# A hybrid decoder layer on one core: modulation and h in two halves of the model's columns, with ten column tiles summed in pairs

## The chip, the cores and the metric

The kernel runs on one core of a Trainium2 chip. The metric is the device time of one execution in microseconds (us). Five engines work side by side and are tied together by semaphores: the tensor engine (PE), VectorE (DVE), ScalarE (ACT), GpSimd (POOL) and SyncE (SP), which issues the transfers from device memory.

## The reference, cut to what matters

```python
shift, scale, gate = jnp.split(c @ w_ada + b_ada, 3, axis=-1)
h = _rmsnorm(x, g_pre) * (1.0 + scale[:, None, :]) + shift[:, None, :]
z_ssm, xbc, dt_raw, q, kv, nsa_gate, z_att, merge_gate = jnp.split(h @ w_in, IN_SPLITS, axis=-1)
y_ssm = _mamba2_branch(z_ssm, xbc, dt_raw, ...) @ w_ssm_out
y_nsa = _nsa_branch(q, kv, nsa_gate, z_att, ...) @ w_nsa_out
mg = jax.nn.sigmoid(merge_gate.reshape(bsz, s, N_BRANCH, dm))
merged = mg[:, :, 0] * y_ssm + mg[:, :, 1] * y_nsa
return x + gate[:, None, :] * _rmsnorm(merged @ w_out, g_post)
```

x has 256 rows of 1024 columns. The Mamba branch passes x, B and C through a causal convolution of four taps, and runs the chunked state-space sum (SSD) over 32 heads in four groups. The attention branch compresses keys and values (kc, vc) in overlapping blocks through a small MLP, and adds a full attention.

## The kernel before

**Units.** Every weight matrix is cut into units of 128 x 1024 floats (512 KB), 133 of them, in the order of `weight_units()` (L35): first dtg (dt and the attention gates), b0 to b3, c0 to c3, then four times four x tiles and four z tiles, then kc0, kc1, vc0, vc1, then za and the weights of the compression (w1k, w1v), and so on. SyncE copies the units one after the other into seven slots w_raw (L492).

**The split.** A product in full precision is made of three faster ones. ScalarE casts a unit to w_hi (L847, `split_hi`), VectorE takes w_raw - w_hi for the first six or seven of the eight pieces (L1096, `split_lo`), and GpSimd for the rest (L1415). h is split likewise into h_hi and h_lo. `weight_unit()` (L572) then gives, for each of the eight pieces k of h's columns, three products: h_hi x w_hi (L621), h_lo x w_hi (L622), h_hi x w_lo (L623). So a unit is 24 products. Splits run three units ahead (`AHEAD`).

**The sums** of a column tile lie in one of three PSUM banks (gemm0 to gemm2) in rotation. Four more kinds of bank exist: score0, score1, small0, small1 and y_or_o.

**The start.** SyncE issues params, the first constants, then the eight pieces of w_ada for shift and scale (L476, 1 MB each, a piece is 128 rows of the model) with x after the second, then two units. The tensor engine sums the squares of x over the columns (L523), multiplies c by each piece as it lands (L531), and transposes the four rows of 512 results (L536), which ScalarE has copied (L934). VectorE makes shift (L1212) and scale (L1214); h is then made piece by piece: h_hi on ScalarE (L939), h on VectorE (L1218) or, for k = 2, 4, 6, on GpSimd (L1405), and h_lo on VectorE (L1226). All eight pieces of w_ada must have landed before any of h exists.

**The order** is written out by hand. `schedule()` (L64) puts named steps behind units; `put(10, ("acs", 0))` puts step acs behind unit 10. The tensor engine and GpSimd follow STEPS, ScalarE and VectorE follow LATE_STEPS, in which the steps behind a unit come one unit later. A finished tile is read out one unit later, too: for b, c and x that is one ScalarE operation (L881), three of VectorE's (L1144), a tanh (L890) and a product (L1105). The steps that count here:

- dtT, dtA, dtE, dtB, dtL, dtC: dt from dtg, in small operations on several engines; GpSimd's last chain is dtC (L1449 to L1457), and acs (L644) on the tensor engine waits for its result, adt.
- xt, seg, ea, y (L700, L703), ysq, ysum, ssq, yn: the SSD of a group and its norm, from unit 17 + 8g on for group g.
- blk (L463, `compress_blocks`): the overlapping blocks of kc on VectorE (behind unit 48) and of vc on GpSimd (behind 47), 16 operations each. The first w1k product (L595) waits for kc's.

## Time and profile before

| | |
|---|---|
| median of 3 runs | 485.87 us (485.31 to 487.09) |
| profiled execution | 486.2 us, its span 484.4 us |
| PE busy | 447.9 us (92%) |
| DVE / ACT / POOL busy | 350.6 / 266.9 / 228.9 us |
| granted clock, mean | 0.981 of full speed |
| moved | 82.99 MB, mean 171 GB/s |

The span runs from the first to the last instruction of the profiled execution. Busy is the time in which an engine had an instruction under way; matmuls overlap, so their own durations (0.28 us) are longer than the distance between two of them. The granted clock tells how much of TensorE's 2.4 GHz was given: 1.00 or 0.50 (1.2 GHz) at any one time.

### The profile page before, as it was taken

Reading aid. Unit: us, or ns where it says so; the run is one execution under the profiler, and the core shown is the slowest. Engines: PE = TensorE matmul, PEld = TensorE weight load, DVE = VectorE, ACT = ScalarE, POOL = GpSimd, SP = SyncE. Lnnn points to the kernel's source line nnn. Section 1 sums busy time; section 2 is a strip of 40 time slices with the busy share of each in tenths; the row PEclk is TensorE's granted clock in tenths of the full one; section 3 lists DMA queues with packets and bytes.
Section 4 is the critical chain, followed back from the end, with each engine's and each line's share of the span. In section 5 each row is a group of like instructions: output and inputs, shape, how many; then the busy total and the mean of one; then the engine's idle time right before and its main releaser. Section 6 shows DMA issues by size and latency. Waiting matters only on the chain.

```text
span 484.4 us, 9763 instructions
## 1 busy us (share of the span) xinstructions
PE 447.9 (92%) x3592; PEld 409.6 (85%) x3592; DVE 350.6 (72%) x611; ACT 266.9 (55%) x518; POOL 228.9 (47%) x238
## 2 busy tenths in 40 slices
PE   0759989999999979997999999999999999999995
PEld 0439989999999879995889999889898999999874
DVE  0167989698999988979775676668696766549633
ACT  1354776555585584635587744656565464535441
POOL 0043453358477746988255552244355353344340
PEclk9987999999999998999999998999999999999999
DMA  8996544733534226144719740625747433356102
GB/s 319 425 385 221 173 132 146 217 117 131 177 127 169 96 93 213 45 175 148 264 62 360 259 169 1 246 76 201 262 140 248 137 101 130 120 178 243 58 2 87
DMA packets 21959, 82.99 MB, mean 171 GB/s; under 512 B 2444, under 2 KB 2834, under 8 KB 20626
## 3 DMA queue, kind: packets, MB, share of 16 engines
q1 hardware_dynamic: 21912, 82.37, 48.1%
q8 instruction: 29, 0.48, 0.4%
q14 instruction: 18, 0.15, 0.1%
HBM read 81.31 MB, written 1.05 MB: 170 GB/s over the span
## 4 chain that ended last, share of the span: by engine, by line
PE 72%; DVE 7%; issue 7%; ACT 5%; DMA 5%; POOL 3%; SPq 1%; DVEq 0%; POOLq 0%; ACTq 0%
PE gemm L621 18%; PE gemm L622 17%; PE gemm L623 17%; DMA w_raw<-in_wpack 5%; PE y_or_o L818 2%; ACT w_hi L847 2%; PE y_or_o L700 2%; ACT probs L1051 1%; DVE w_lo L1096 1%; PE score L782 1%; DVE cmp_blocks L463 1%; PE score L784 1%; SPq L476 1%; PE small L568 1%; PE small L570 1%
## 5 line engine op out<-in xcount | busy, mean ns | idle before, releaser
L1415 POOL TENSOR_TENSOR w_lo<-w_raw,w_hi 128x256 fp32r<-128x256 f32 (+1 forms) x117 | 128.5, 1104 | 171.5 <-ACT w_hi L847 137.4
L621 PE MATMUL gemm<-h_hi,w_hi 128*128 128x256 f32 x680 | 198.1, 291 | 2.4 <-DVE h_lo L1226 2.1
L622 PE MATMUL gemm<-h_lo,w_hi 128*128 128x256 f32 x680 | 192.8, 284 | 0.0
L623 PE MATMUL gemm<-h_hi,w_lo 128*128 128x256 f32 x680 | 192.4, 283 | 0.0
L1096 DVE TENSOR_TENSOR w_lo<-w_raw,w_hi 128x768 fp32r<-128x768 f32 (+1 forms) x117 | 128.9, 1103 | 42.5 <-ACT w_hi L847 41.9
L847 ACT CAST w_hi<-w_raw 128x1024 fp32r<-128x1024 f32 x117 | 122.1, 1045 | 41.8 <-PE gemm L623 27.7
L621 PEld LDWEIGHTS gemm<-h_hi,w_hi 128*128 128x128 f32 x680 | 130.6, 192 | 5.7 <-issue 4.7
L622 PEld LDWEIGHTS gemm<-h_lo,w_hi 128*128 128x128 f32 x680 | 130.6, 192 | 0.6
L623 PEld LDWEIGHTS gemm<-h_hi,w_lo 128*128 128x128 f32 x680 | 130.4, 192 | 0.0
L1144 DVE SCALAR_TENSOR_TENSOR conv_acc<-gemm,conv_half,conv_acc 128x255 f32<-128x255 f32 (+2 forms) x72 | 34.5, 480 | 8.2 <-ACT conv_acc L881 6.2
L621 PE MATMUL gemm<-ynorm_hi,w_hi 128*128 128x256 f32 x128 | 36.6, 286 | 0.0
L623 PE MATMUL gemm<-ynorm_hi,w_lo 128*128 128x256 f32 x128 | 35.8, 280 | 0.0
L622 PE MATMUL gemm<-ynorm_lo,w_hi 128*128 128x256 f32 x128 | 35.8, 279 | 0.0
L881 ACT ACTIVATE conv_acc<-gemm,conv_half 128x256 f32<-128x256 f32 x24 | 13.6, 565 | 32.2 <-PE gemm L623 21.2
L1051 ACT ACTIVATE probs<-score,softmax_small 128x128 f32<-128x128 f32 (+1 forms) x64 | 26.1, 423 | 1.5 <-DVE softmax_small L1333 1.5
L1467 POOL TENSOR_TENSOR cb_decay<-decay,cb_T 128x512 f32<-128x512 f32 x8 | 13.0, 1629 | 27.0 <-ACT decay L990 27.0
L621 PEld LDWEIGHTS gemm<-ynorm_hi,w_hi 128*128 128x128 f32 x128 | 24.0, 188 | 0.7 <-issue 0.7
L1425 POOL TENSOR_TENSOR seg_moving<-acs_rows,consts 128x512 fp32r<-128x512 f32 x16 | 21.7, 1375 | 6.1 <-DVE acs_cols L1259 6.1
L622 PEld LDWEIGHTS gemm<-ynorm_lo,w_hi 128*128 128x128 f32 x128 | 24.1, 188 | 0.0
L623 PEld LDWEIGHTS gemm<-ynorm_hi,w_lo 128*128 128x128 f32 x128 | 24.0, 188 | 0.0
L854 ACT ACTIVATE tanh_tmp<-gemm 128x256 f32<-128x256 f32 x24 | 9.2, 385 | 23.6 <-PE gemm L623 22.8
L1058 ACT COPY probs_T<-small 128x512 f32<-128x512 f32 x16 | 9.5, 593 | 20.6 <-PE y_or_o L818 20.5
(233 smaller groups left out, 778.8 us busy)
## 6 DMA issues: line engine op xcount, KB each, us to landing
w_raw<-in_wpack SPq DMA_DIRECT2D x133, 512.0 KB, 4.0
w_ada_shift_scale<-in_w_ada SPq DMA_DIRECT2D x8, 1024.0 KB, 14.8
x_T<-in_xT SPq DMA_DIRECT2D x1, 1024.0 KB, 10.4
x_residual<-in_x_tok SPq DMA_DIRECT2D x1, 1024.0 KB, 4.9
out_tok_dram<-out_tok SPq DMA_DIRECT2D x4, 256.0 KB, 2.1
...
```

Source lines behind the costliest of these rows:

```text
L621: nc.tensor.matmul(bank[:, 0:SEQ], w_hi, hi[:, k0 + k, :], start=first, stop=False)
L622: nc.tensor.matmul(bank[:, 0:SEQ], w_hi, lo[:, k0 + k, :], start=False, stop=False)
L623: last = nc.tensor.matmul(bank[:, 0:SEQ], w_lo, hi[:, k0 + k, :], start=False, stop=end)
L700: nc.tensor.matmul(bank[64 * k:64 * k + 64, CHUNK * c:CHUNK * (c + 1)], XDT[:, c, h, :], MM[:, c, q4, :], start=True, stop=(c == 0))
L847: nc.scalar.copy(WH[:, n % HI_SLOTS, :], RAW[:, u % RAW_SLOTS, :]).then_inc(hi_ready, 1)
L881: nc.scalar.activation(ACC[:, ci % 2, :], bank, ACT.Identity, bias=CW[:, 96 + col:97 + col], scale=CW[:, 4 * col + 3:4 * col + 4]).then_in ...
L1051: last = nc.scalar.activation(E[:, k, b, P * qt:P * qt + nk], SB[qt][:, nk * b:nk * b + nk], ACT.Exp, bias=SM[:, k, 0, c:c + 1], accum_out ...
L1096: nc.vector.tensor_tensor(WL[:, n % LO_SLOTS, 0:c], RAW[:, u % RAW_SLOTS, 0:c], WH[:, n % HI_SLOTS, 0:c], ALU.subtract).then_inc(lo_ready, 1)
L1144: ins = nc.vector.scalar_tensor_tensor(ACC[:, ci % 2, s:SEQ], GB[t % G_BANKS][:, 0:SEQ - s], CW[:, 4 * col + tap:4 * col + tap + 1], ACC[: ...
L1415: nc.gpsimd.tensor_tensor(WL[:, n % LO_SLOTS, c:1024], RAW[:, u % RAW_SLOTS, c:1024], WH[:, n % HI_SLOTS, c:1024], ALU.subtract).then_inc( ...
L1425: nc.gpsimd.tensor_tensor(MV[:, c, :, :], TP[:, c, :].unsqueeze(1).to_broadcast([P, 4, P]), oh, ALU.mult).then_inc(mv_done, 1)
L1467: nc.gpsimd.tensor_tensor(MM[:, 1, :, :], EX[:, 1, :, :], CB[:, 1, i // 2, :].unsqueeze(1).to_broadcast([P, 4, P]), ALU.mult).then_inc(mm_ ...
```

## The change

Modulation and h are made in two halves of the model's 1024 columns, 512 each. w_ada is laid out so that the first 4 MB give shift and scale of the first half, the second 4 MB those of the second. The squares, the scaling of x, the row sums (32 products of 256 columns for each half, into a half bank of small0), the copy, the transposes and h each come as two calls.

Ten tiles (dtg, b0 to b3, c0, kc0, kc1, vc0, vc1) are taken in five pairs. A pair unit holds for two tiles the weights of one half of the columns: 24 products as in any unit, twelve for each tile. Units 0 to 4 are the pairs' first halves, units 5 to 9 their second halves; their ten sums stay open meanwhile in all banks but small0 (`HOME`, two tiles in one bank where there is a 1). The second half of the modulation (step ada2) stands behind unit 3, its transposes in the middle of unit 4. Then come c1, c2, c3 (units 10 to 12), and x and z from 13 on, four units later than before; kc and vc no longer stand behind the last z. The SSD steps come three units later. The dt steps move too, the blocks of kc and vc are made group by group behind units 18 + 8g (kc, VectorE) and 19 + 8g (vc, GpSimd). In units 5 to 16 a split goes ahead of the read-outs. SyncE issues x first, then alternates. Of h, GpSimd makes k = 2 and 6 only, VectorE k = 4 too. The exponential of a_log and the three casts of constants (L1399 to L1401) move behind other work; the transfer of alibi_k no longer waits for the norm. The number of units, products with h, and bytes is the same.

```diff
+PAIRS = ((("dtg", 0), ("b", 0)), (("kc", 0), ("b", 1)), (("kc", 1), ("b", 2)), (("vc", 0), ("b", 3)), (("vc", 1), ("c", 0)))
+PAIR_READ = (PAIRS[0], (("b", 1),), (("kc", 0), ("kc", 1), ("b", 2)), (("b", 3),), (("vc", 0), ("vc", 1), ("c", 0)))
+HALF_K = KT // 2
+
+
 def weight_units():
 
-    units = [("dtg", 0, 0)]
-    units += [("b", j, 0) for j in range(4)] + [("c", j, 0) for j in range(4)]
+    units = [("pair", i, half) for half in range(2) for i in range(len(PAIRS))]
+    units += [("c", j, 0) for j in range(1, 4)]
     for g in range(SSM_GROUPS):
         units += [("x", TPG * g + j, 0) for j in range(TPG)] + [("z", TPG * g + j, 0) for j in range(TPG)]
-    units += [("kc", j, 0) for j in range(2)] + [("vc", j, 0) for j in range(2)]
-
     units += [("za", j, 0) for j in range(6)]
...
+def tiles_done(u):
+
+    kind, j, part = UNITS[u]
+    if part != LAST_PART.get(kind, 0):
+        return ()
+    return PAIR_READ[j] if kind == "pair" else ((kind, j),)
...
-    put(2, ("dtT", 0))
-    put(4, ("dtA", 0), ("dtE", 0))
-    put(6, ("dtB", 0), ("dtL", 0))
-    put(8, ("dtC", 0))
-    put(10, ("acs", 0))
+    put(len(PAIRS) - 2, ("ada2", 0))
+    put(6, ("dtT", 0))
+    put(7, ("dtA", 0), ("dtE", 0))
+    put(8, ("dtB", 0), ("dtL", 0))
+    put(10, ("dtC", 0))
+    put(13, ("acs", 0))
     for kind in range(3):
-        put(11 + kind, ("cb", kind))
+        put(15 + kind, ("cb", kind))
     ssq_after = 12
     for g in range(SSM_GROUPS):
-        b = 17 + 8 * g
+        b = 20 + 8 * g
...
-    put(47, ("blk", 1))
-    put(48, ("blk", 0))
+    for g in range(KV_GROUPS):
+        put(18 + 8 * g, ("blk0", g))
+        put(19 + 8 * g, ("blk1", g))
+    put(47, ("clear", 0))
...
+HOME = {("dtg", 0): ("gemm0", 0), ("b", 0): ("gemm0", 1), ("b", 1): ("gemm1", 0), ("b", 2): ("gemm2", 0),
+        ("b", 3): ("score0", 0), ("c", 0): ("score1", 0), ("kc", 0): ("small1", 0), ("kc", 1): ("small1", 1),
+        ("vc", 0): ("y_or_o", 0), ("vc", 1): ("y_or_o", 1)}
+SECOND_HALVES = [tile for tile in HOME if HOME[tile][1]]
+FIRST_HALVES = [tile for tile in HOME if tile not in SECOND_HALVES and (HOME[tile][0], 1) in HOME.values()]
+BEFORE, _n = {}, 0
+for _tile in TILE_IDX:
+    if _tile not in HOME:
+        HOME[_tile] = (BANKS[_n % G_BANKS], 0)
+        _n += 1
+    _last = [t for t in TILE_IDX if TILE_IDX[t] < TILE_IDX[_tile] and HOME[t][0] == HOME[_tile][0]]
+    BEFORE[_tile] = _last[-2:] if _last and HOME[_last[-1]][1] == 1 else _last[-1:]
 RAW_SLOTS, HI_SLOTS, LO_SLOTS = 7, 4, 4
-H_POOL = (2, 4, 6)
+H_POOL = (2, 6)
+H_DVE = tuple(k for k in range(KT) if k not in H_POOL)
+EARLY_SPLITS = range(len(PAIRS), 17)
...
-            for k in range(KT):
-                sp.dma_start(ADA[:, k, :], w_ada1[:, k, :]).then_inc(ada_in[k], 16)
-                if k == 1:
-                    sp.dma_start(XT[:], xT).then_inc(x_in, 16)
-            for u in range(2):
-                sp.dma_start(RAW[:, u, :], wpack[u]).then_inc(w_in[u], 16)
+            for s in range(2):
+                sp.dma_start(XT[:, HALF_K * s:HALF_K * (s + 1), :], xT[:, HALF_K * s:HALF_K * (s + 1), :]).then_inc(x_in[s], 16)
+            first_units = len(PAIRS)
+            for n in range(KT):
+                s, k = n // HALF_K, 2 * (n % HALF_K)
+                if n >= HALF_K - 1:
+                    u = n - HALF_K + 1
+                    sp.dma_start(RAW[:, u, :], wpack[u]).then_inc(w_in[u], 16)
+                sp.dma_start(ADA[:, s, k:k + 2, :], w_ada1[:, s, k:k + 2, :]).then_inc(ada_in[n], 16)
             sp.dma_start(CS[:, early:CST["end"][1]], cst_in[:, early:CST["end"][1]]).then_inc(cst2_in_s, 16)
-            for u in range(2, len(UNITS)):
+            for u in range(first_units, len(UNITS)):
...
+            def ada_rows(s):
+
+                for k in range(KT):
+                    if k % 2 == 0:
+                        pe.wait_ge(ada_in[HALF_K * s + k // 2], 16)
+                    for j in range(4):
+                        last = nc.tensor.matmul(ada_sums[32 * j:32 * j + 1, :], par("c", k, k + 1),
+                                                ADA[:, s, k, 256 * j:256 * j + 256], start=(k == 0), stop=(k == KT - 1))
+                last.then_inc(ada_full, 1)
+
+            def ada_columns(s):
+
+                pe.wait_ge(rows_done, s + 1)
+                for m in range(2):
+                    o = 256 * s + P * m
+                    last = nc.tensor.transpose(ada_cols[:, P * m:P * m + P], ROWS[:, o:o + P], ident)
+                last.then_inc(modT_full, 1)
+
             pe.wait_ge(par_in_s, 16)
             pe.wait_ge(bank_zeroed, 1)
-            for k in range(KT):
-                pe.wait_ge(ada_in[k], 16)
-                for j in range(4):
-                    last = nc.tensor.matmul(SB[0][32 * j:32 * j + 1, :], par("c", k, k + 1), ADA[:, k, 512 * j:512 * j + 512],
-                                            start=(k == 0), stop=(k == KT - 1))
-            last.then_inc(ada_full, 1)
-            pe.wait_ge(rows_done, 1)
-            for m in range(4):
-                last = nc.tensor.transpose(SB[1][:, P * m:P * m + P], ROWS[:, P * m:P * m + P], ident)
-            last.then_inc(modT_full, 1)
+            ada_rows(0)
+            ada_columns(0)
...
+                if kind == "pair":
+                    n = SPLIT_IDX[u]
+                    pe.wait_ge(hi_ready, n + 1)
+                    pe.wait_ge(lo_ready, n + 1)
+                    for kk in range(HALF_K):
+                        k = HALF_K * part + kk
+                        if j == 0:
+                            pe.wait_ge(h_ready, k + 1)
+                        if u == len(PAIRS) - 1 and kk == 2:
+                            ada_columns(1)
+                        for m in range(2):
+                            c = 2 * kk + m
+                            if c == lo_share(n):
+                                pe.wait_ge(lo_rest_ready, n + 1)
+                            bank = home(PAIRS[j][m])
+                            w_hi = WH[:, n % HI_SLOTS, P * c:P * c + P]
+                            w_lo = WL[:, n % LO_SLOTS, P * c:P * c + P]
+                            first = k == 0 and PAIRS[j][m] not in SECOND_HALVES
+                            end = k == KT - 1 and PAIRS[j][m] not in FIRST_HALVES
+                            nc.tensor.matmul(bank, w_hi, HH[:, k, :], start=first, stop=False)
+                            nc.tensor.matmul(bank, w_hi, HL[:, k, :], start=False, stop=False)
+                            last = nc.tensor.matmul(bank, w_lo, HH[:, k, :], start=False, stop=end)
+                    last.then_inc(unit_mm, 1)
...
+                elif what == "ada2":
+                    ada_rows(1)
...
+            copy_rows(0)
             split_hi(1)
-
...
+                    split_first = i in EARLY_SPLITS or any(kind == "nsa" for kind, j in done)
+                    if not split_first:
+                        for tile in done:
+                            read_out(tile)
                     if i + AHEAD in SPLIT_IDX:
                         split_hi(SPLIT_IDX[i + AHEAD])
-                    if not late_split:
-                        read_out(done)
-                    done = finished_tile(i)
+                    if split_first:
+                        for tile in done:
+                            read_out(tile)
...
+            scale_x(0)
             split_lo(0)
-
-            dve.wait_ge(modT_full, 1)
-            rows = SB[1][:, :].rearrange("p (m j r) -> p j m r", m=4, j=4)[:, :, :, 0]
-            link(nc.vector.tensor_tensor(MOD[:].rearrange("p (j m) -> p j m", j=4), rows,
-                                         par("b_ada", 0, 16).rearrange("p (j m) -> p j m", j=4), ALU.add))
-            nc.vector.scalar_tensor_tensor(AB[:, 0:8], MOD[:, 8:16], 1.0, par("g_pre"), ALU.add, ALU.mult).then_inc(ab_done, 1)
-            dve.wait_ge(ab_done, 1)
-            for k in range(KT):
-                if k not in H_POOL:
-                    nc.vector.tensor_scalar(HF[:, k, :], XT[:, k, :], AB[:, k:k + 1], MOD[:, k:k + 1], ALU.mult,
-                                            ALU.add).then_inc(h_f32, 1)
-                if k >= 1:
-                    dve.wait_ge(h_hi, k)
-                    if k - 1 in H_POOL:
-                        dve.wait_ge(h_f32_pool, H_POOL.index(k - 1) + 1)
-                    else:
-                        dve.wait_ge(h_f32, k - sum(m < k - 1 for m in H_POOL))
-                    nc.vector.tensor_tensor(HL[:, k - 1, :], HF[:, k - 1, :], HH[:, k - 1, :], ALU.subtract).then_inc(h_ready, 1)
-            dve.wait_ge(h_hi, KT)
-            dve.wait_ge(h_f32, KT - len(H_POOL))
-            nc.vector.tensor_tensor(HL[:, KT - 1, :], HF[:, KT - 1, :], HH[:, KT - 1, :], ALU.subtract).then_inc(h_ready, 1)
-            for n in range(1, AHEAD):
+            make_h(0)
+            split_lo(1)
+            scale_x(1)
+            for n in range(2, AHEAD):
...
+                elif what == "blk1":
+                    pool.wait_ge(lo_rest_ready, made_rest[0])
+                    compress_blocks(pool, nc.gpsimd, 1, i)
+                elif what == "clear":
                     nc.gpsimd.memset(HVR[:], 0.0).then_inc(zeros, 1)
```

**The tensor engine's queue at the start.** First before, the last piece of w_ada and unit 0; then after, where units 3 and 4 meet and unit 5 begins. w_raw, w_hi, w_lo are the weights, small0, score1 and so on are PSUM banks.

```order
L531 MATMUL score0<-w_ada_shift_scale_84,params_60 1x512 [waits ada_in7]
L531 MATMUL score0<-w_ada_shift_scale_84,params_60 1x512 x3
L536 MATMUL score1<-consts_61,ada_rows_89 128x128 [waits rows]
L536 MATMUL score1<-consts_61,ada_rows_89 128x128 x3
L621 MATMUL gemm0<-h_hi_53,w_hi_57 128x256 [waits h_ready,lo_ready,hi_ready]
```

```order
L655 MATMUL score0<-h_hi_53,w_lo_58 128x256
L575 MATMUL small0<-w_ada_shift_scale_84,params_60 1x256 [waits ada_in4]
...
L575 MATMUL small0<-w_ada_shift_scale_84,params_60 1x256 [waits ada_in7]
L575 MATMUL small0<-w_ada_shift_scale_84,params_60 1x256 x7
L653 MATMUL y_or_o<-h_hi_53,w_hi_57 128x256 [waits lo_ready,hi_ready]
...
L655 MATMUL score1<-h_hi_53,w_lo_58 128x256
L584 MATMUL small0<-consts_61,ada_rows_89 128x128 [waits rows]
L584 MATMUL small0<-consts_61,ada_rows_89 128x128
...
L653 MATMUL gemm0<-h_hi_53,w_hi_57 128x256 [waits h_ready,lo_ready,hi_ready]
```

The sums of w_ada's second half, which stood ahead of every product with h, now stand in the stream of such products, and 12 products lie between the second transposes and unit 5.

**SyncE's queue at the start,** before and after.

```order
L473 DMA params_60<-in_params 128x297
L474 DMA consts_61<-in_consts 128x256
L476 DMA w_ada_shift_scale_84<-in_w_ada1 128x2048 x2
L478 DMA x_T_85<-in_xT 128x2048
L476 DMA w_ada_shift_scale_84<-in_w_ada1 128x2048 x6
L480 DMA w_raw_55<-in_wpack 128x1024 x2
```

```order
L514 DMA params_60<-in_params 128x297
L515 DMA consts_61<-in_consts 128x256
L517 DMA x_T_85<-in_xT 128x1024 x2
L524 DMA w_ada_shift_scale_84<-in_w_ada1 128x2048 x3
L523 DMA w_raw_55<-in_wpack 128x1024
L524 DMA w_ada_shift_scale_84<-in_w_ada1 128x2048
L523 DMA w_raw_55<-in_wpack 128x1024
L524 DMA w_ada_shift_scale_84<-in_w_ada1 128x2048
```

x stands ahead of w_ada, the first unit ahead of its fourth piece, and each later piece has a unit in front of it.

**VectorE's queue where the blocks of kc are made,** before (behind the last z tiles) and after (here the last of four places, between two z tiles).

```order
L1280 SCALAR_TENSOR_TENSOR x_conv_T_90<-x_conv_T_90,params_60,y_or_o 128x256 x2
L1285 TENSOR_TENSOR z_gate_then_y_76<-x_conv_T_90,z_gate_then_y_76 128x512
L463 TENSOR_TENSOR cmp_blocks_104<-kv_cmp_T_105,params_60 64x8x15 x16
L1105 SCALAR_TENSOR_TENSOR z_att_then_o_79<-tanh_tmp_109,gemm1 128x256
L1298 TENSOR_TENSOR ynorm_lo_78<-y_tmp_102,ynorm_hi_77 128x256
```

```order
L1412 RECIPROCAL rstd_y_103<-rstd_y_103 128x256
L1417 SCALAR_TENSOR_TENSOR y_tmp_102<-z_gate_then_y_76,params_60,rstd_y_103 128x256
L504 TENSOR_TENSOR cmp_blocks_104<-kv_cmp_T_105,params_60 64x8x15 x4
L1202 SCALAR_TENSOR_TENSOR z_gate_then_y_76<-tanh_tmp_109,gemm0 128x256
L1193 TENSOR_TENSOR w_lo_58<-w_raw_55,w_hi_57 128x768
```

Sixteen operations in one lump have become four times four, among the read-outs of the z tiles.

## Rows read from the trace of the kernel before

**Rows 1.** The page, part 1: busy us (share of the span) and instructions by engine.

```profile
PE 447.9 (92%) x3592; PEld 409.6 (85%) x3592; DVE 350.6 (72%) x611; ACT 266.9 (55%) x518; POOL 228.9 (47%) x238
```

**Rows 2.** Windows: us of the window, busy us (instructions) by engine, clock, DMA share, GB/s.

```profile
core 0: us, PE busy (x) PEld busy (x) DVE busy (x) ACT busy (x) POOL busy (x), PEclk, DMA share, GB/s
0.00:33.30 33.30, 13.27 (x84) 6.08 (x84) 7.42 (x11) 8.91 (x11) 2.90 (x13) 0.98 0.95 382
33.30:42.40 9.10, 8.76 (x35) 7.97 (x36) 9.10 (x14) 5.97 (x10) 5.66 (x7) 0.50 0.60 222
```

**Rows 3.** Transfers of w_ada: size and number; issues of first and last; issue to landing.

```profile
w_ada_shift_scale<-in_w_ada SPq DMA_DIRECT2D x8, 1024.0 KB, 14.8
...
1.65 0.42 SPq L476
6.59 0.45 SPq L476
...
DMA to landing us min/median/max: 6.4/14.8/21.3
```

**Rows 4.** Timeline of the start: start us, us, engine, line, operation, idle before and its releaser.

```profile
27.98 1.04 PE L531 MATMUL score<-w_ada_shift_scale,params 128*1 128x512 f32 x8 [1.34 <-DMA w_ada_shift_scale<-in_w_ada]
29.25 1.04 ACT L847 CAST w_hi<-w_raw 128x1024 fp32r<-128x1024 f32 x1 [6.87 <-DMA w_raw<-in_wpack]
30.84 0.66 PE L536 MATMUL score<-consts,ada_rows 128*128 128x128 f32 x4 [1.81 <-ACT ada_rows L934]
31.53 0.17 DVE L1212 TENSOR_TENSOR mod<-score,params 128x16 f32<-128x16 f32 x1 [0.17 <-PE score L536]
31.94 4.04 ACT L939 ACTIVATE h_hi<-x_T,mod,ada_scale 128x256 fp32r<-128x256 f32 x8 [0.21 <-DVE ada_scale L1214]
33.35 0.55 PE L621 MATMUL gemm<-h_hi,w_hi 128*128 128x256 f32 x1 [1.86 <-DVE h_lo L1226]
35.03 1.82 DVE L1226 TENSOR_TENSOR h_lo<-h,h_hi 128x256 fp32r<-128x256 f32 x2
```

**Rows 5.** Chain of waits, start us and us: products, 81 between the last two rows.

```profile
41.36 0.21 PE gemm L623
...
47.01 0.22 PE small L635 x2
...
54.30 0.12 PE gemm L621
...
63.84 0.12 PE gemm L621
```

**Rows 6.** The tensor engine's waits after 33 us: us in total, times, longest.

```profile
PE y_or_o L700 <- POOL cb_decay_across L1484: 2.3, 1, 2.3
PE small L644 <- POOL adt L1457: 1.8, 1, 1.8
PE gemm L595 <- DVE cmp_blocks L463: 1.7, 1, 1.7
PE small L710 <- POOL y_sq L1479: 1.5, 1, 1.5
PE gemm L621 <- DVE w_lo L1096: 0.2, 1, 0.2
```

**Rows 7.** Chain of waits: eight short records, two column groups side by side.

```profile
213.93 0.44 PE y_or_o L700 x8
```

**Rows 8.** Timeline of GpSimd: first and last operation of dtC.

```profile
66.67 0.55 POOL L1449 TENSOR_SCALAR dt<-dt_work 128x64 f32<-128x64 f32 x1
70.05 1.57 POOL L1457 TENSOR_SCALAR adt<-dt_work 128x256 f32<-128x256 f32 x1
```

**Rows 9.** Windows in the SSD stretch, columns as in rows 2.

```profile
100.00:130.00 30.00, 30.00 (x268) 28.43 (x267) 26.61 (x41) 17.41 (x30) 19.16 (x16) 1.00 0.44 151
130.00:160.00 30.00, 30.00 (x266) 28.23 (x265) 28.17 (x43) 20.73 (x34) 20.67 (x18) 1.00 0.41 141
160.00:200.00 40.00, 37.24 (x310) 35.05 (x309) 36.32 (x49) 23.54 (x40) 28.08 (x23) 0.96 0.35 119
```

**Rows 10.** VectorE's blocks: duration ns min/median/max, first and last start.

```profile
L463 DVE TENSOR_TENSOR cmp_blocks<-kv_cmp_T,params x16: 340/364/544, 216.3 to 221.6; 64x120 f32<-64x120 f32 x16
```

258 lines of the change are left out of this document (160 added, 98 removed).

## The prediction, made before the changed kernel ran

> **What bounds the kernel now.** I read the page's busy shares first, then the stages, then the chain of waits stage by stage. The tensor engine is busy 447.9 of 484.4 us [rows 1], so the time falls only where its idle time falls, where its clock rises, or where work leaves it. The reader should add up where the 36.5 us of idle time lie: 20 of them (33.3 less 13.27 busy) come before the first product with h [rows 2]; four waits of 1.5 to 2.3 us make 7.3 [rows 6]; most of the rest is the tail, which the change leaves alone. So the start decides.
>
> The start is bound by transfers. Up to 33.3 us they move 382 GB/s [rows 2], and all eight 1 MB pieces of the modulation weights stand ahead of the first product. The first piece was issued at 1.65 and landed 6.4 us later, at 8.05; the last was issued at 6.59 and landed 21.3 us later, at 27.89 [rows 3]. Between the two landings lie seven more pieces and x, 8 MB in 19.84 us: **2.48 us per MB**, and transfers land in the order of issue. Behind the last landing come sums (27.98), transposes (30.84), modulation (31.53), h on ScalarE (31.94) and the first product (33.35): 5.4 us of chain [rows 4]. Then the granted clock is 0.50, the 1.2 GHz level, until 42.4 us [rows 2].
>
> **The change, part by part.**
>
> *a. The first product comes earlier.* Ahead of the last piece of the first half stand params, constants, x, four pieces and one weight unit. That is 4.5 MB more than stood ahead of the first piece's landing before: 8.05 + 4.5 x 2.48 = 19.2 us. From there the chain is as before but without the 1.04 us cast at 29.25 that ran on ScalarE in front of the row copy [rows 4] (its unit now lands at 16.7), and with one small VectorE operation of 0.2 more: two k sums 0.9, copy 0.4 (half of the columns), two transposes 0.35, three small operations 0.65, h 1.4 (31.94 to 33.35), with 0.3 for handing over. That makes **23.2 us, -10.1**.
>
> *b. The slow stretch.* Before, 33.35 to 47.23 us held three units (72 products) and two transposes [rows 4, 5]. At full pace a product takes (63.84 - 54.30)/81 = 0.118 us [rows 5], so this would be 72 x 0.118 + 0.22 = 8.7; it took 13.9, 5.2 too much, from the half clock and from waiting for h piece by piece. Afterwards each k of h feeds six products of 0.213 us [rows 5], 1.28 us, and VectorE delivers a k every 0.4 to 0.9 us (two h_lo in 1.82 us at the slowest [rows 4]), so the engine doesn't starve. Before, the engine did 0.66 us of work between 29.0 and 33.35, and then showed the lower clock; now it does 0.35 between 20.1 and 23.2, and I take it that the clock falls again. How long it stays down is bounded by 0 below and by the 9.1 us of before above; unbroken work speaks for about half of that, 5.1 us. It costs 5.1 x (1 - 0.118/0.213) = 2.3 (0 to 4.1). **-2.9.**
>
> *c. The second half of the modulation moves onto the tensor engine's path.* Its sums lay under the transfers before; now they stand between units 3 and 4. Four units at 24 products end at about 36.8 (23.2 + 96 x 0.118 + 2.3); the last piece lands 6 MB after 19.2, at 34.1, so it doesn't hold them up. They are 32 products, 64 records. Before, 56 records with 512 columns took 6.19 us, 0.11 each; with 256 columns, half, if columns set it. The nearest short records that run side by side in column groups, eight in 0.44 us, 0.055 each [rows 7], bear that out. So 64 x 0.055 = **+3.5**; the upper bound is 64 x 0.11 = 7.0. Then two transposes, **+0.3**, in the middle of unit 4. From the end of these to the next product with new h is 1.85 (31.50 to 33.35) + 0.2; 12 products (1.4) cover it, so it leaves **+0.6**. ScalarE's cast of unit 7 stands ahead of the second row copy: that unit lands at 34.1 + 1.75 MB, 38.4, and is cast by 39.5, while the sums end at 40.3. That is a margin of 0.8; a later landing goes straight onto the path.
>
> The Trainium skill, in "TensorE: Matmul & The Clock Gate", under the back-to-back issue gap, puts the sustained spacing of load and product at about 81 ns for 128 columns. By that the sums would be at least 64 x 0.081 = 5.2, and the forecast 1.7 later. Here the trace's 0.055 decides.
>
> *d. Three waits go.* The wait of 1.8 us for adt at L644 [rows 6]: GpSimd's last chain took from 66.67 to 71.62 [rows 8], and the tensor engine was there at 69.8, two units after that chain could start. Now dtC stands after unit 10 and acs after unit 13, so three units (8.5 us) lie between them where two did, and the split goes ahead of the read-outs on ScalarE. **-1.8.** The waits for the key blocks (1.7) and for y_sq behind GpSimd's blocks (1.5) [rows 6] arise because 16 operations stood in one lump; the blocks now come in fours, long before w1k. **-1.7, -1.5.**
>
> *e. VectorE gets the key blocks in its fullest stretch.* Four operations of 0.364 us [rows 10] per group, 1.46 us. It is busy 26.6 of 30, 28.2 of 30 and 36.3 of 40 us there [rows 9]: room for the first two groups, none for the last two. **+2.9** (0 to 5.8).
>
> *At nothing:* h's piece 4 goes from GpSimd to VectorE (0.41 us) under the six products per k; the three casts of constants on GpSimd move behind h; the square root's table is loaded during the wait for x; the exp of a_log stands in ScalarE's gaps. The order of banks costs nothing as long as read-outs keep within three units. The later SSD ends tens of units ahead of the products that need it, and its own steps are the same in number. If that cover went, it would show as waits for gemm banks.
>
> Sum: -10.1 - 2.9 + 3.5 + 0.3 + 0.6 - 5.0 + 2.9 = **-10.7**. The profiled execution took 486.2, so 475.5; the median of the runs is 0.3 lower, so **475.2 us**.
>
> **Rivals.**
> - *VectorE sets the pace in the SSD stretch.* All four groups pay (5.8, 2.9 more than in e), and the 1.8 of adt is time that VectorE needed to catch up, so it reappears at y_or_o. For it: 28.2 of 30. Against: the tensor engine waited for a split of VectorE's for 0.2 us in all [rows 6]. 475.2 + 4.7 = 479.9.
> - *Better than forecast.* The clock does not fall during the shorter pauses (-2.3), and the 2.3 us wait at L700 [rows 6], a coincidence of four engines' order, does not come again. 470.6. For it: the mean clock up to 33.3 us was 0.98, through gaps of 1.3 and 1.8 us [rows 2, 4].
> - *Slower: transfers pace the pair units.* Between two units' weights now stands 1 MB of modulation, so units land 1.5 MB or 3.7 us apart, against 2.8 us of work at full clock. If the tensor engine waits in front of each, its clock stays at the low level, and all 240 products up to unit 9 take 0.213: 240 x 0.095 = 22.8 instead of 2.3, giving 495.7. It decides against the change from 10.7/0.095, some 113 more slow products (nearly five units). Against: units 1 to 4 land at 20.4, 24.1, 27.8 and 31.6, each well ahead of its turn when unit 0 starts at 23.2.
> - *The change does not start the kernel earlier,* because the queued transfers share the engines and the first half lands with the second. Then a is 0, and c is hidden: 485 or so. Against: the landings in order [rows 3].
>
> **Chances.** Forecast 0.68; VectorE sets the pace 0.15; better 0.11; transfers pace the pairs 0.03; no earlier start 0.03. The range takes in both middle rivals and the bounds of c and e that don't coincide: 470 to 481. A measurement of this kernel tells about 0.5%, 2.4 us, from no change. Faster by more: all but the last two, 0.94; within it 0.03; slower 0.03.
>
> **What would show it.** The first product with h at 23.2 +- 1; the sums of the second half taking about 3.5 us right after unit 3; the first product of unit 5 at 44; end of unit 5 near 47 (55.5 before). No waits at adt, cmp_blocks and y_sq; VectorE over 95% busy between 120 and 190 us. I am wrong if the clock in the profile is 0.50 beyond 33 us, if units 1 to 4 wait for w_raw, or if a wait above 3 us appears at y_or_o or score.

## The result: faster by 0.9%, and 6.3 us short of the forecast

The changed kernel took **481.54 us** (median, 480.88 to 482.9), the kernel before 486.15 beside it: ratio 0.9912, 95% interval [0.9888, 0.9937]. A second comparison gave 482.0 against 486.11, 0.9915 [0.9896, 0.9934]. One execution of experiment 4, the one that was profiled, ran at a granted clock of 0.75 throughout and took 554.41 us, and it is left out of the figures below. The forecast was 475.2 us with a range of 470 to 481; the direction was right, the size less than half of what was forecast, and the range missed it by half a microsecond.

The profiled execution spans 480.3 us (484.4 before). The page, part 1, beside [rows 1]:

```profile
PE 449.0 (93%) x3656; PEld 412.0 (86%) x3656; DVE 352.9 (73%) x617; ACT 266.3 (55%) x520; POOL 231.1 (48%) x237
```

TensorE is busy 1.1 us longer, in a span that is 4.1 us shorter. So the idle time fell by 5.2, and the work itself took longer. The clock has a part in that, as will be seen.

**The start.** The timeline of TensorE, beside [rows 4]:

```profile
19.88 1.89 PE L575 MATMUL small<-w_ada_shift_scale,params 128*1 128x256 f32 x16 [2.72 <-DMA w_ada_shift_scale<-in_w_ada]
22.25 0.69 PE L584 MATMUL small<-consts,ada_rows 128*128 128x128 f32 x2 [0.49 <-ACT ada_rows L1019]
25.48 0.55 PE L653 MATMUL gemm<-h_hi,w_hi 128*128 128x256 f32 x1 [2.54 <-DVE h_lo L1316]
...
38.39 3.63 PE L575 MATMUL small<-w_ada_shift_scale,params 128*1 128x256 f32 x64
...
45.91 0.36 PE L653 MATMUL gemm<-h_hi,w_hi 128*128 128x256 f32 x1 [0.69 <-DVE h_lo L1316]
```

The fourth piece landed at 19.88 (forecast 19.2). In the 2.72 us for which TensorE waited for it the clock fell (it reads 0.50 from 18.4 to 28.7 us), so its 16 sums took 1.89 us; at full clock they take 1.04 (experiment 3). The first product with h came at 25.48, not 23.2. Windows around it:

```profile
16.00:23.00 7.00, 3.62 (x34) 0.99 (x34) 2.27 (x4) 2.22 (x3) 1.50 (x1) 0.67 1.02 418
23.00:29.00 6.00, 3.52 (x18) 3.55 (x18) 5.86 (x13) 3.46 (x7) 3.76 (x3) 0.53 1.02 419
29.00:33.00 4.00, 4.00 (x36) 4.00 (x35) 2.50 (x2) 1.31 (x2) 1.13 (x2) 1.00 1.02 412
```

From 28.7 us on the clock is 1.00: 3.2 us of products at the 1.2 GHz level, where [rows 2] show 9.1. The low stretch itself is as long as before, 10.2 us (32.3 to 42.5 us there); it only began sooner before the first product, so that most of it lies under the waits, the sums and the transposes. The second half's 64 sums stood right behind unit 3 and took 3.6 us; unit 5 began at 45.91 (forecast 44), and the next one at 48.98 (55.5 before; forecast 47).

**Waits behind the start.** TensorE's waits from 49 us on, beside [rows 6]:

```profile
PE y_or_o L782 <- POOL cb_decay_across L1613: 5.0, 2, 4.1
PE small L799 <- DVE cmp_hidden L1202: 2.4, 2, 1.7
PE gemm L694 <- DVE conv_acc L1240: 1.0, 2, 0.7
PE score L864 <- ACT probs L1148: 0.7, 3, 0.2
PE small L619 <- issue: 0.6, 1, 0.6
PE gemm L694 <- DVE w_lo L1193: 0.4, 1, 0.4
```

The three waits that were to go (adt, the key blocks, y_sq; 5.0 us) are gone. In their place the one at y_or_o grew from 2.3 to 5.0, that for cmp_hidden from 0.8 to 2.4, and conv_acc's of 1.0 is new. The whole list sums to 10.1 us; that of before, from 56 us on, to 10.8.

**The clock behind the start.** Windows of 20 us, first of the kernel before, then of the changed one (the clock is the third figure from the end):

```profile
180.00:200.00 20.00, 18.23 (x148) 17.45 (x149) 17.84 (x22) 10.67 (x19) 14.98 (x13) 0.91 0.46 159
240.00:260.00 20.00, 18.99 (x160) 18.57 (x160) 13.38 (x23) 14.63 (x32) 10.65 (x9) 1.00 0.46 163
280.00:300.00 20.00, 19.76 (x154) 18.76 (x152) 12.86 (x27) 9.52 (x28) 6.20 (x7) 0.91 0.24 81
```

```profile
180.00:200.00 20.00, 15.93 (x129) 14.96 (x128) 19.40 (x28) 12.13 (x23) 13.81 (x15) 0.91 0.39 132
240.00:260.00 20.00, 20.00 (x160) 20.00 (x159) 13.35 (x24) 16.73 (x36) 13.79 (x11) 0.91 0.51 190
280.00:300.00 20.00, 19.86 (x146) 19.34 (x144) 13.77 (x31) 7.22 (x22) 5.54 (x7) 0.83 0.13 47
```

Narrower windows give 3.4 us at the 0.50 level for each 0.91 and 6.8 for the 0.83. So behind the start the kernel before spends 6.8 us at the low level, the changed one 13.7 (the other windows show 1.00 up to 460 us). A product takes 0.213 us there and 0.118 at the high level, so 45% of such a stretch is lost: 3.0 us more than before. The mean clock of the changed kernel's ten runs is 0.976, of the kernel before 0.983; that takes in the start too, so it doesn't tell where the clock was low.

The account of the profiled spans: start -6.5, waits behind it 10.1 - 10.8 = -0.7, clock behind it +3.0, in sum -4.2 where -4.1 was measured.

**The same kernel, profiled a second time.** The second comparison's trace (span 481.0) divides the loss otherwise:

```profile
20.54 1.89 PE L575 MATMUL small<-w_ada_shift_scale,params 128*1 128x256 f32 x16 [2.73 <-DMA w_ada_shift_scale<-in_w_ada]
...
180.00:200.00 20.00, 15.94 (x124) 15.00 (x123) 19.40 (x30) 13.12 (x23) 12.58 (x13) 0.83 0.42 139
240.00:260.00 20.00, 18.15 (x150) 17.74 (x151) 12.81 (x23) 17.01 (x37) 12.55 (x9) 1.00 0.38 138
280.00:300.00 20.00, 19.78 (x154) 18.95 (x154) 13.84 (x32) 8.45 (x23) 6.76 (x10) 0.91 0.16 53
```

The piece landed 0.7 us later, the first product with h came at 26.15, the clock stayed at 0.50 until 32.0, and the unit behind unit 5 began at 50.90 in place of 48.98: start -4.6. The waits behind it sum to 11.3, +0.5. Behind the start the clock was low for 10.2 us, 1.9 of them inside the wait at y_or_o, where they cost nothing; the other 8.3, against 6.8 before, cost +0.7. In sum -3.4, and -3.4 was measured. So the start was worth 4.6 to 6.5 us and the clock behind it cost 0.7 to 3.0, depending on the execution.

**Where the long wait comes from.** Timeline of ScalarE and GpSimd ahead of the 4.1 us for which y waited up to 185.6:

```profile
171.18 0.56 ACT L962 ACTIVATE conv_acc<-gemm,conv_half 128x256 f32<-128x256 f32 x1 [2.76 <-DVE x_conv_T L1202]
175.38 0.56 ACT L962 ACTIVATE conv_acc<-gemm,conv_half 128x256 f32<-128x256 f32 x1 [2.40 <-DVE x_conv_T L1202]
...
177.21 1.28 ACT L1103 ACT_TABLE_LOAD   x1
...
179.00 1.28 ACT L1087 ACT_TABLE_LOAD   x1
180.29 1.09 ACT L1087 ACTIVATE decay<-score 128x512 f32<-128x512 f32 x2
...
181.46 1.28 POOL L1596 TENSOR_TENSOR cb_decay<-decay,cb_T 128x512 f32<-128x512 f32 x1 [7.61 <-ACT decay L1087]
...
183.46 1.89 POOL L1613 TENSOR_TENSOR cb_decay_across<-decay_across,cb_T 128x512 f32<-128x512 f32 x1
```

Read it backwards: y needs cb_decay_across, GpSimd waited 7.61 us for the decay, the decay stands behind two table loads on ScalarE, and ScalarE had waited 5.2 us for VectorE's x_conv_T. VectorE was behind. Its windows, beside [rows 9]:

```profile
130.00:160.00 30.00, 30.00 (x265) 28.14 (x264) 29.55 (x44) 19.08 (x31) 22.83 (x22) 1.00 0.40 130
160.00:200.00 40.00, 35.00 (x291) 32.91 (x290) 39.05 (x58) 24.33 (x42) 23.99 (x24) 0.96 0.38 129
```

Two theories follow. **V**: VectorE's key blocks in its fullest stretch are the loss. **C**: the stretch is a chain of four in-order queues with no slack, and whatever is shifted comes back as a wait elsewhere. On the start: **S**, the landing and ScalarE's order set the first product; and **K**, the clock costs what it seems to.

### The profile page after: what moved, and what is told of

Read it like the earlier page. It is cut to its first block, busy times and chain, and to the rows that moved or that the text cites. A ratio compares the mean times of both kernels' runs of the same rounds, so it can differ in the third digit from the quotient of the medians.

```text
span 480.3 us, 9912 instructions
## 1 busy us (share of the span) xinstructions
PE 449.0 (93%) x3656; PEld 412.0 (86%) x3656; DVE 352.9 (73%) x617; ACT 266.3 (55%) x520; POOL 231.1 (48%) x237
## 4 chain that ended last, share of the span: by engine, by line
PE 69%; DVE 9%; issue 9%; POOL 5%; ACT 4%; DMA 3%; SPq 1%; DVEq 0%; ACTq 0%; POOLq 0%
PE gemm L694 15%; PE gemm L696 15%; PE gemm L695 15%; DMA w_ada_shift_scale<-in_w_ada 3%; PE y_or_o L900 2%; DVE w_lo L1193 2%; DVE conv_acc L1240 2%; ACT w_hi L929 2%; POOL w_lo L1535 2%; POOL seg_moving L1547 1%; PE score L864 1%; PE small L575 1%; PE y_or_o L782 1%; PE score L866 1%; PE gemm L653 1%
## 5 line engine op out<-in xcount | busy, mean ns | idle before, releaser
L1535 POOL TENSOR_TENSOR w_lo<-w_raw,w_hi 128x256 fp32r<-128x256 f32 (+1 forms) x117 | 131.9, 1133 | 181.5 <-ACT w_hi L929 147.7
L694 PE MATMUL gemm<-h_hi,w_hi 128*128 128x256 f32 x600 | 174.4, 291 | 1.5 <-DVE conv_acc L1240 1.0
L695 PE MATMUL gemm<-h_lo,w_hi 128*128 128x256 f32 x600 | 169.8, 283 | 0.0
L696 PE MATMUL gemm<-h_hi,w_lo 128*128 128x256 f32 x600 | 169.7, 283 | 0.0
L1193 DVE TENSOR_TENSOR w_lo<-w_raw,w_hi 128x768 fp32r<-128x768 f32 (+1 forms) x117 | 131.3, 1123 | 44.9 <-ACT w_hi L929 44.0
L694 PEld LDWEIGHTS gemm<-h_hi,w_hi 128*128 128x128 f32 x600 | 115.1, 192 | 3.9 <-issue 2.4
L695 PEld LDWEIGHTS gemm<-h_lo,w_hi 128*128 128x128 f32 x600 | 114.8, 191 | 0.6
L696 PEld LDWEIGHTS gemm<-h_hi,w_lo 128*128 128x128 f32 x600 | 114.6, 191 | 0.0
L1240 DVE SCALAR_TENSOR_TENSOR conv_acc<-gemm,conv_half,conv_acc 128x255 f32<-128x255 f32 (+2 forms) x66 | 31.6, 479 | 3.3 <-ACT conv_acc L962 1.7
L962 ACT ACTIVATE conv_acc<-gemm,conv_half 128x256 f32<-128x256 f32 x22 | 12.4, 564 | 25.2 <-DVE x_conv_T L1202 14.1
```

Source lines behind the costliest of these rows:

```text
L694: nc.tensor.matmul(bank[:, 0:SEQ], w_hi, hi[:, k0 + k, :], start=first, stop=False)
L695: nc.tensor.matmul(bank[:, 0:SEQ], w_hi, lo[:, k0 + k, :], start=False, stop=False)
L696: last = nc.tensor.matmul(bank[:, 0:SEQ], w_lo, hi[:, k0 + k, :], start=False, stop=end)
L962: nc.scalar.activation(ACC[:, ci % 2, :], bank, ACT.Identity, bias=CW[:, 96 + col:97 + col], scale=CW[:, 4 * col + 3:4 * col + 4]).then_in ...
L1193: nc.vector.tensor_tensor(WL[:, n % LO_SLOTS, 0:c], RAW[:, u % RAW_SLOTS, 0:c], WH[:, n % HI_SLOTS, 0:c], ALU.subtract).then_inc(lo_ready, 1)
L1240: ins = nc.vector.scalar_tensor_tensor(ACC[:, ci % 2, s:SEQ], bank[:, 0:SEQ - s], CW[:, 4 * col + tap:4 * col + tap + 1], ACC[:, ci % 2, s ...
```

## The experiments

Each is an edit of the changed kernel, timed beside the kernel before. The changed kernel's own ratios were 0.9912 and 0.9915.

**1. All blocks in lumps again, behind 47 and 48.**

```diff
-    for g in range(KV_GROUPS):
-        put(18 + 8 * g, ("blk0", g))
-        put(19 + 8 * g, ("blk1", g))
-    put(47, ("clear", 0))
+    put(47, *[("blk1", g) for g in range(KV_GROUPS)])
+    put(48, *[("blk0", g) for g in range(KV_GROUPS)], ("clear", 0))
```

> Undoes one part of the change: the blocks of kc (VectorE) and vc (GpSimd) go back into one lump each behind units 48 and 47. Theory V (VectorE sets the pace of the SSD stretch, and the 1.46 us of blocks per group pushed it over): VectorE is busy under 37.5 of 40 us between 160 and 200 us (39.05 in the changed kernel), the waits at y_or_o fall from 5.0 us to 3 or less, and the waits at cmp_blocks (1.7) and y_sq (1.5) come back, so that the total moves by -1.5 to +1.5 us against the changed kernel. Rival D (the wait at y_or_o comes from the SSD standing one unit nearer to its x tiles, blocks or not): the waits at y_or_o stay at 5 us, and with the lump's waits back the kernel is about 3 us slower than the changed one.

486.24 us, ratio 1.0011 [0.9992, 1.003]: 4.7 slower than the changed kernel. The SSD now ends behind unit 51, so the lump on GpSimd stood ahead of its last cb_decay:

```profile
PE y_or_o L780 <- POOL cb_decay_across L1611: 8.7, 2, 5.9
```

5.9 of the 8.7 us is that lump; the other 2.8 us stand where the changed kernel waits 5.0. So spreading them is worth 4.7 us here, and the blocks inside the stretch lengthen its wait by 2.2.

**2. The SSD one unit later** (`b = 21 + 8 * g`).

> The SSD steps of every group stand one unit later (21 + 8g in place of 20 + 8g), as far behind their x tiles as before the change; the blocks stay spread. Theory V: VectorE has the same work for the same stretch, so the sum of the waits at y_or_o stays near 5 us and the time within 1 us of the changed kernel. Rival D (distance): the waits at y_or_o fall to about 2.3 us, as before the change, and the kernel is 2 to 3 us faster than the changed one.

483.07 us, 0.9937 [0.9918, 0.9956]. Waits at y_or_o 5.3: more distance doesn't help. All waits behind the start sum to 11.8.

**3. The last piece of the first half ahead of unit 0's weights** in the transfer queue.

```diff
+                sp.dma_start(ADA[:, s, k:k + 2, :], w_ada1[:, s, k:k + 2, :]).then_inc(ada_in[n], 16)
                 if n >= HALF_K - 1:
...
-                sp.dma_start(ADA[:, s, k:k + 2, :], w_ada1[:, s, k:k + 2, :]).then_inc(ada_in[n], 16)
```

> In SyncE's queue each piece of w_ada goes ahead of the weight unit that stood in front of it. The fourth piece should land 1.24 us earlier (18.6 in place of 19.9) and unit 0 that much later. Theory L (the landing of the fourth piece bounds the start): first product with h at 24.2 or, if the clock then does not fall in the shorter gap, at 23; the kernel is 1 to 2 us faster than the changed one. Rival S (the split of unit 0 takes its place): unit 0 lands at 19.9, is cast by 21.2 and split by 22.2, GpSimd's rest by 22.8, in time for h; only if the first product stays at 25.5 is this rival right, and the time stays.

482.53 us, 0.9924 [0.9905, 0.9942]: not faster. The sums started at 18.89 and ran at full clock (1.04 us), but ScalarE has casts of weight units in front of the row copy and of h:

```profile
20.14 1.04 ACT L929 CAST w_hi<-w_raw 128x1024 fp32r<-128x1024 f32 x1 [4.84 <-DMA w_raw<-in_wpack]
...
23.91 1.04 ACT L929 CAST w_hi<-w_raw 128x1024 fp32r<-128x1024 f32 x1 [2.44 <-DMA w_raw<-in_wpack]
24.86 2.07 ACT L1025 ACTIVATE h_hi<-x_T,mod,ada_scale 128x256 fp32r<-128x256 f32 x4
```

The cast of unit 1 waited for its landing with h queued behind it, and the first product came at 26.19, no earlier than without the edit (25.48 and 26.15 in the two profiles of the changed kernel).

**4. Eight products on constants in TensorE's waits at the start**, four ahead of the last two k of the sums and four behind the transposes; their sums are read by nobody.

> Eight products of constants into an unused bank are added, four in the tensor engine's wait for the fourth piece of w_ada, four behind the first transposes. They add work of no use, about 2.6 us in each place, where the engine waits 2.7 and 2.5 us. Theory C (2.3 us were missed at the start because the clock fell at 18.7 us, during the wait for the fourth piece): granted clock 1.00 throughout, sums of the fourth piece in 0.9 us in place of 1.9, first product with h 1.4 us earlier at 24.1, no slow stretch (3.4 us at 1.2 GHz, worth 1.5 us), end of unit 5 at 46 in place of 48.8, kernel 2 to 3 us faster than the changed one. Rival: if the vector and scalar engines set the start, the clock stays up and the first product moves by less than 0.5 us, the kernel by under 1.5 us.

480.39 us, 0.9886 [0.9867, 0.9905], some 1.3 below the changed kernel by the ratios, at the edge of what can be told, and less than the 2 to 3 us that theory C of this expectation (K above) gave. The runs' mean clock rose from 0.976 to 0.987. Where the first product came is not known of this edit alone; experiment 12 shows the start with these products in it.

**5. VectorE's blocks behind units 45 to 48**, GpSimd's as in the change.

```diff
-        put(18 + 8 * g, ("blk0", g))
+        put(45 + g, ("blk0", g))
...
-    put(47, ("clear", 0))
+    put(50, ("clear", 0))
```

> Of the 32 key-block operations, VectorE's 16 leave the SSD stretch and follow units 45 to 48, one group each; GpSimd's 16 stay where the change put them. Theory V (VectorE's load in the SSD stretch makes the waits at y_or_o): its busy time between 100 and 200 us falls by about 5.8 us, the waits at L782 fall from 5.0 to 2 or less, and the time is 2.5 to 3.5 us below the changed kernel's. Theory O (the order of one in-order queue, the norm's two table loads ahead of the last decay on ScalarE, makes the wait): the long wait of 4.1 us shrinks only by what VectorE's backlog put in front of it, the gain is 0 to 1.5 us. If the new place is too late for the first product of w1k, a wait at the blocks of 1 us or more shows there.

480.52 us, 0.9883 [0.9864, 0.9902], 1.5 below the changed kernel.

```profile
PE y_or_o L782 <- POOL cb_decay_across L1613: 2.9, 1, 2.9
...
PE gemm L670 <- DVE cmp_blocks L504: 1.9, 1, 1.9
```

V is right that the blocks lengthen the wait at y_or_o (5.0 to 2.9), and C is right that they pay elsewhere: 1.9 us at w1k's first product.

**6. The norm's statistics one place later** (`ssq_after = 13`), so that the last decay stands ahead of the two table loads.

> The norm's squares and statistics go one place later in the order, so that the decay of the last group stands ahead of the two table loads on ScalarE. Theory O: the wait of 4.1 us at L782 falls to about 1.5 (the two loads, 2.6 us, leave the way), time 1.5 to 2.6 us below the changed kernel's, unless the norm's own reader then waits. Theory V: VectorE is as full as before, the wait comes back within 1 us at another place, time within 1 us of the changed kernel's.

485.89 us, 1.0002 [0.9982, 1.0021]. The wait of 4.1 fell to 2.4, but there are five now, 8.0 us in sum. The two loads now stand ahead of decay_across (L1093) in the place of decay. My theory of a single bad place (O) falls.

**7. The hidden rows' transposes one unit later.**

> The two transposes of the compressor's hidden rows and the copy behind them go one unit later. If they are a wait of their own (VectorE's reciprocal of 1.7 us ahead of what they read), the 2.4 us at L799 go and the time is 1.5 to 2.5 us below the changed kernel's, more if the low clock that follows at 240 us goes with them. If they only take up slack that would show at the next reader (the k_hi cast or the scores), the waits at L799 go, but the time stays within 0.7 us.

483.06 us, 0.9941 [0.9921, 0.9961], 1.3 slower. The 2.4 us at L799 went, and 4.8 came behind it: 2.1 for VectorE's k_lo, 1.7 for w_lo, 1.0 for a w_hi of ScalarE's.

**8. Edit 3 with h_hi ahead of the cast of unit 1 on ScalarE.**

```diff
             copy_rows(0)
+            make_h_hi(0)
             split_hi(1)
-            make_h_hi(0)
```

> On the transfer queue the last piece of the first half goes ahead of unit 0's weights, and on ScalarE h_hi(0) goes ahead of the cast of unit 1. Theory S (in e3 the gain of the earlier landing was lost in ScalarE's order): the first product with h comes at 24.0 to 24.6 us (25.5 in the changed kernel, 26.2 in e3), the slow stretch starts and ends earlier by the same, the time is 0.8 to 1.6 us below the changed kernel's. Rival (unit 0's weights, now landing later, or the split of unit 1 hold the pair units up): first product at 25 or later, or waits for the casts of unit 1 of 0.5 us or more; time within 0.5 us of the changed kernel's or above.

480.37 us, 0.9897 [0.9878, 0.9916]. The first product came at 23.89 and unit 5 at 44.38 (45.91; 47.84 in the second profile), as S says. By the ratios 0.8 us of these 1.6 reached the time, within the error of the comparison; the profiled spans (478.6 against 480.3) show all of it.

**9. VectorE's blocks ahead of the SSD, behind units 10, 12, 14 and 16** (acs_hi moved to memory that is free then).

> VectorE's 16 key-block operations follow units 10, 12, 14 and 16, ahead of the SSD, where VectorE is busy 23.4 of 28 us, and not units 18, 26, 34 and 42. Theory V (their 5.8 us in the SSD stretch are the loss): VectorE's busy time between 100 and 200 us falls by 4 to 5 us, the waits at L782 fall from 5.0 us to 3 or less, no wait at the blocks arises (as it did with them late, 1.9 us), time 2.5 to 4.5 us below the changed kernel's. Rival C (the long waits are a coincidence of four queues' order that any shift reshuffles): the waits at L782 and L799 sum to 5 us or more again, and the time is within 1.5 us of the changed kernel's.

482.42 us, 0.9929 [0.9909, 0.9949], 0.7 slower than the changed kernel. The waits at y_or_o fell to 2.8 again; but c_T now waited for 1.5 and conv_acc for 2.5 (1.0), between 75 and 100 us. VectorE had no room there either.

**10. Edits 4, 8 and 9 together.**

> e9's two orders, e10's places and the 8 constant products of the earlier experiment on the clock together. If their gains add (theories S and V): 4 to 7 us below the changed kernel's, 475 to 477.5 us. If each only moves slack to the next place (rival C): 479 to 481 us.

482.65 us, 0.994 [0.9921, 0.9959]: the early blocks took back all that 4 and 8 gained.

**11. All 32 blocks on GpSimd**, VectorE's 16 behind units 26, 34, 42 and 47.

```diff
-        put(18 + 8 * g, ("blk0", g))
+        put(min(26 + 8 * g, 47), ("blk0", g))
...
-    put(47, ("clear", 0))
+    put(50, ("clear", 0))
...
-                elif what == "blk0":
-                    compress_blocks(dve, nc.vector, 0, i)
...
+                elif what == "blk0":
+                    pool.wait_ge(lo_rest_ready, made_rest[0])
+                    compress_blocks(pool, nc.gpsimd, 0, i)
```

> VectorE's 16 key-block operations go to GpSimd, four each behind units 26, 34, 42 and 47, one in a stretch where GpSimd waits 3.5 us for ScalarE's decay. Theory V (VectorE's own load is the loss): its busy time from 75 to 200 us falls from 120.9 to 113 or less (before: 111.2), the waits at L782 fall from 5.0 us to 1.5 or less, no wait at the blocks, time 3 to 4.5 us below the changed kernel's. Rival P (GpSimd's operations stretch VectorE's while both run: w_lo of 128x896 took 0.95 us at its shortest and 1.25 in the middle; before, 1.09): VectorE's busy time falls by 3 us or less, the waits at L782 stay at 3 us or more, time within 1.5 us of the changed kernel's. Rival C (any shift reshuffles the waits): busy time falls as V says, but the waits come back elsewhere, and the time is within 1.5 us.

**478.56 us**, 0.985 [0.9835, 0.9866]: 3.1 below the changed kernel by the ratios, which is the time that V gave. But the waits are not what gave it:

```profile
PE y_or_o L782 <- POOL cb_decay_across L1611: 3.5, 2, 2.8
...
75.00:200.00 125.00, 121.43 (x1055) 115.45 (x1054) 118.34 (x177) 76.37 (x127) 91.68 (x93) 1.00 0.42 140
180.00:200.00 20.00, 17.15 (x153) 16.36 (x152) 19.82 (x29) 11.39 (x21) 19.12 (x20) 1.00 0.41 133
...
280.00:300.00 20.00, 18.35 (x146) 16.72 (x146) 15.15 (x36) 9.17 (x26) 3.91 (x5) 1.00 0.20 71
```

Between 75 and 200 us VectorE's busy time fell from 120.86 to 118.34 us only, which looks like rival P. But this kernel gets further in the same 125 us (1055 of TensorE's records against 1026). From the first x tile's gate to the end of the last one's, 834 records in both, the changed kernel and this one show:

```profile
84.00:182.60 98.60, 96.39 (x834) 91.32 (x834) 95.12 (x145) 60.99 (x100) 63.77 (x64) 1.00 0.44 145
83.20:179.90 96.70, 96.12 (x834) 91.16 (x834) 90.58 (x133) 60.88 (x100) 69.20 (x72) 1.00 0.44 148
```

VectorE has 12 operations less, the 12 blocks of this stretch, and is busy 4.5 us less, of the 5.4 that they took. So it was relieved, as V says; what P said of VectorE's busy time falls, though its 3 us or more at L782 came true. The waits at y_or_o fell by 1.5, not 3.5; but the wait for probs grew by 1.0, y_sq's by 0.6, and all waits behind the start sum to 11.2 (10.1 and 11.3 in the changed kernel), as C says. What is left is the start (0.7 earlier than in the first profile) and the clock: 1.00 at 180 and at 280 us, low for 3.4 us behind the start, and a mean of 0.987 over its runs (0.976 in the changed kernel). Whether the edit keeps the clock up, and how, isn't shown.

**12. Edits 4 and 8 alone.**

> The two orders of e9 and the 8 constant products, nothing else. Theory S and the clock together: no slow stretch between 18 and 31 us, first product with h at 23.7 to 24.2, unit 6 starts at 46.5 to 47.3 (48.98 in the changed kernel), and the time is 2 to 3 us below the changed kernel's, 478.5 to 479.5 us. Rival C: the front comes earlier as said, but the time is within 1 us of the changed kernel's.

480.21 us, 0.9889 [0.9867, 0.9912]. The clock is 1.00 from 15 to 47 us, the first product came at 24.13 and unit 5 at 44.83; the gain, 1.2 us by the ratios, is no more than that of edit 4 alone.

**13. Edits 4, 8 and 11 together.**

> All blocks on GpSimd, the two orders of e9 and the 8 constant products together. If the gains add: 475 to 477.5 us, ratio 0.977 to 0.982. If the waits of the middle only move: 478.5 to 480.5.

**477.0 us** (476.87 to 479.38), 0.9825 [0.9807, 0.9844]: the fastest, 8.5 us below the kernel before and 4.3 below the changed one. Unit 5 began at 44.02. The waits behind the start sum to 10.0, as many as in the changed kernel: the gain is the start and the clock. The clock is 1.00 from 15 to 47 us. Behind that it shows what is still not controlled:

```profile
180.00:200.00 20.00, 17.95 (x146) 17.18 (x147) 19.01 (x25) 10.34 (x19) 19.14 (x20) 0.91 0.51 152
...
280.00:300.00 20.00, 19.39 (x148) 18.36 (x148) 15.18 (x35) 9.87 (x28) 3.79 (x5) 0.91 0.21 77
```

The same wait of 2.8 us at y_or_o is followed by a slow stretch here and was not in experiment 11. What decides that isn't shown.

**14 and 15. On top of 13: the SSD one unit earlier; or the hidden rows one unit later.**

> e13 with the SSD one unit earlier. Theory T (the SSD's last norm now falls on the compressor's hidden rows: reciprocal and table loads ahead of them): the waits at cmp_hidden's transposes fall from 2.5 us to 1.5 or less, and the time is 1 to 2 us below e13's 477.0. Rival C: the waits at y_or_o or conv_acc grow by as much (x_conv_T is one unit nearer to its reader), time within 0.8 us of e13's or above.

> e13 with the hidden rows' transposes one unit later. Alone this cost 1.1 us (the waits went to k_lo and w_lo). If VectorE's relief has made room there: the waits at cmp_hidden go, those at k_lo and w_lo stay under 1 us, time 1 to 2 us below 477.0. If the waits belong to that stretch's order and not to VectorE's load: 2 us or more at k_lo and w_lo again, time 477 to 478.5.

478.0 us, 0.9862 [0.9836, 0.9889], and 480.91 us, 0.9892 [0.987, 0.9914]. The first took 1.0 us off the waits at cmp_hidden (T is right about their origin), and its profile shows a clock of 1.00 from 180 to 300 us; but waits at y_sq (1.4, new), seg_moving (1.2, from 0.4) and probs (1.7, from 1.1) ate it up, and the time is no better, as rival C of that expectation says. The second brought back 2.1 at k_lo and 1.0 at w_lo, though VectorE has the blocks no more: these belong to the order of that stretch. Its time is above both ranges of its expectation.

## Why the prediction was wrong, step by step

Three steps failed: where the clock falls at the start (a), what was put at nothing, and the clock behind the start, for which there was no term. b, c, d and e held or nearly so.

*a, the first product: -10.1 forecast, -7.9 measured.* The mechanism held (half as many bytes ahead of it); the sizes did not. The landing was 0.7 late (1.3 in the second profile), the sums 1.0 slower at the low clock, the transposes 0.3, and h's own chain the rest. The failed step is the sentence that the clock falls "between 20.1 and 23.2": it had fallen at 18.4, before the sums, in the wait for the piece. Experiment 8 took 1.6 us off the first product (2.3 against the second profile), with the piece earlier and h first in ScalarE's queue; experiment 3, with the piece alone, took off nothing.

*b, the slow stretch: 5.1 us assumed, 3.2 measured* (25.48 to 28.7), 0.9 us better than forecast; 5.9 in the second profile, 0.4 worse.

*c, the second half: +4.4 forecast.* The sums took 3.6 (3.5 forecast), so the trace's 0.055 per record was right: 0.057 here. The Trainium skill gives some 81 ns at 128 columns in "TensorE: Matmul & The Clock Gate", under the back-to-back issue gap; these products, with 256 columns in four column groups, stayed below it. The wait for the new h was 0.7 (0.6). Both hold. Start in sum: -8.6 forecast, -6.5 measured; **2.1 of the miss** (4.0 in the second profile).

*d, three waits go: -5.0.* They went. Experiment 1, with the lumps back, brought back the 1.7 for the key blocks; for adt's new place no run stands alone.

*e, the blocks: +2.9.* The size held, for a reason that was incomplete. It priced eight operations at 0.364 us, and all 16 took 7.19 us in the stretch, 0.45 each. With the blocks out of it (experiments 1 and 5) the waits at y_or_o are 2.8 and 2.9 in place of 5.0: they cost 2.1 to 2.2 us there. The cost does not stay on VectorE: in the timeline above it is handed on by the in-order queues from VectorE to ScalarE to GpSimd to TensorE.

*At nothing: the later SSD and the read-outs.* This step failed. The wait for cmp_hidden grew by 1.6: the last norm, three units later, now meets the compressor's hidden rows (experiment 14, with the SSD one unit earlier, took 1.0 off it). The wait of 1.0 for conv_acc, which is one for a gemm bank, is new and stays in experiments 1 and 5, so it isn't the blocks' doing either. d, e and what stood at nothing together: -2.1 forecast, -0.7 measured; **1.4 of the miss** (+0.5 measured, 2.6 of the miss, in the second profile). The rival "VectorE sets the pace" gave 479.9, the nearest of all to 481.5, but by luck: it wanted 7.6 us of new time there (5.8 of the blocks, 1.8 of adt's wait), and the waits at y_or_o grew by 2.7.

*Not in the sum at all: the clock behind the start, +3.0* (+0.7 in the second profile). The prediction treated the clock as a matter of the first 42 us. This step failed too. With the sums and transposes of a (+1.3) and with b (-0.9, +0.4) the clock makes 3.4 of the miss in the first profile, the largest piece there, and 2.4 in the second, a third of it. The three fastest kernels, 13, 14 and 11, have mean clocks of 0.992, 0.992 and 0.987; it isn't all (experiments 12 and 10 had 0.988, with 480.2 and 482.65 us). What sets off the slow stretches is open. No run removed one behind the start on purpose, and with the same wait ahead it sometimes comes and sometimes does not. What stood ahead of the one at 280 us is in the last section.

2.1 + 1.4 + 3.0 = 6.5, against the 6.6 by which the profiled span (480.3) missed the forecast's (484.4 - 10.7 = 473.7). In the second profile it is 4.0 + 2.6 + 0.7 = 7.3, all of the miss. The range failed for the same reasons: it held bounds for c and e, and none for the clock beyond the start or for the steps that stood at nothing. One of its rivals was summed wrongly: with no earlier start, a and c at 0 and b left out, its terms give 486.2 - 0.3 - 5.0 + 2.9 = 483.8, not "485 or so".
